# Weights' slots and rows of rounded activations at many places modulo 512 bytes, rows as separate buffers

## What is computed

```python
def swiglu(u, w_gate, w_up, w_down):
    return (jax.nn.silu(u @ w_gate) * (u @ w_up)) @ w_down
for l in range(DEPTH):                      # 2
    x = x + 0.5 * g1 * swiglu(modulate(x, sh1, sc1), ffn1_gate[l], ffn1_up[l], ffn1_down[l])
    x = x + g2 * token_mix(modulate(x, sh2, sc2), cos, sin, w_in[l], ...)
    x = x + 0.5 * g3 * swiglu(modulate(x, sh3, sc3), ffn2_gate[l], ffn2_up[l], ffn2_down[l])
# then hybrid_layer: z = h @ w_in + b_in; four branches; merged @ w_o; relu(h2 @ w_up)**2 @ w_down
```

## Time and profile before

| | |
|---|---|
| median of 3 runs | 3470.61 us (3468.10 to 3471.58) |
| span of the profiled execution, first to last instruction | 3462.0 us |
| median less that span | 8.6 us |
| PE busy, share of the span | 99% |
| DVE, ACT, POOL busy | 51%, 35%, 8% |

### The profile page before, as it was taken

One profiled execution on the slowest core, in us unless ns is written; L12 is line 12 of the kernel. 1 busy time (PEld: TensorE's weight loads), 2 busy tenths in 40 slices (PEclk: granted clock), 3 DMA queues, 4 the chain that ended last, 5 costly groups with the idle time before them and its releaser, 6 DMA issues.

```text
span 3462.0 us, 40836 instructions
## 1 busy us (share of the span) xinstructions
PE 3417.4 (99%) x16686; PEld 2737.1 (79%) x16686; DVE 1754.0 (51%) x3014; ACT 1197.3 (35%) x2021; POOL 263.1 (8%) x219
## 2 busy tenths in 40 slices
PE   8999999999999999999999999999999999999999
PEld 7888786778888788887767888888778777878887
DVE  7666446555565733334655643334453555364433
ACT  3222336543222332223555332224322444233322
POOL 0000210002000200011100100003011000120000
PEclk9999999999999999999999999999999999999999
DMA  7555322123565532323211322322222223122332
GB/s 253 203 208 192 108 84 69 41 71 112 190 228 194 183 100 95 104 86 117 74 44 31 105 90 83 106 87 96 77 79 68 76 67 122 39 96 90 98 103 79
DMA packets 120361, 376.36 MB, mean 109 GB/s; under 512 B 13296, under 2 KB 28272, under 8 KB 120176
## 3 DMA queue, kind: packets, MB, share of 16 engines
q1 hardware_dynamic: 120176, 373.76, 32.8%
HBM read 371.61 MB, written 2.10 MB: 108 GB/s over the span
## 4 chain that ended last, share of the span: by engine, by line
PE 93%; DVE 4%; ACT 2%; issue 0%; DMA 0%; POOL 0%; SPq 0%; DVEq 0%; ACTq 0%; POOLq 0%
PE ps L449 27%; PE ps L451 26%; PE ps L450 26%; PE ps L671 2%; PE ps L694 2%; PE ps L566 2%; PE ps L483 1%; PE ps L485 1%; PE ps L484 1%; PE ps L499 1%; DVE s_wl L1490 1%; PE ps L492 1%; ACT s_wh L969 0%; PE ps L536 0%; PE ps L537 0%
## 5 line engine op out<-in xcount | busy, mean ns | idle before, releaser
L1490 DVE TENSOR_TENSOR s_wl<-s_raw,s_wh 128x1024 fp32r<-128x1024 f32 (+3 forms) x645 | 705.7, 1095 | 885.2 <-ACT s_wh L969 878.7
L449 PE MATMUL ps<-s_uh,s_wh 128*128 128x512 f32 x2824 | 1128.5, 400 | 9.7 <-DVE s_ul L1551 3.8
L451 PE MATMUL ps<-s_ul,s_wh 128*128 128x512 f32 x2824 | 1104.2, 391 | 0.8 <-issue 0.8
L450 PE MATMUL ps<-s_uh,s_wl 128*128 128x512 f32 x2824 | 1103.4, 391 | 0.0
L969 ACT ACTIVATE s_wh<-s_raw 128x1024 fp32r<-128x1024 f32 (+3 forms) x645 | 588.1, 913 | 723.0 <-PE ps L451 535.4
L449 PEld LDWEIGHTS ps<-s_uh,s_wh 128*128 128x128 f32 x2824 | 532.2, 188 | 152.8 <-issue 40.2
L451 PEld LDWEIGHTS ps<-s_ul,s_wh 128*128 128x128 f32 x2824 | 531.7, 188 | 113.6 <-issue 1.2
L450 PEld LDWEIGHTS ps<-s_uh,s_wl 128*128 128x128 f32 x2824 | 532.5, 189 | 107.3 <-issue 2.7
L449 PE MATMUL ps<-s_fh,s_wh 128*128 128x512 f32 x960 | 378.6, 394 | 0.0
L451 PE MATMUL ps<-s_fl,s_wh 128*128 128x512 f32 x960 | 378.6, 394 | 0.0
L450 PE MATMUL ps<-s_fh,s_wl 128*128 128x512 f32 x960 | 378.6, 394 | 0.0
(11 more groups left out here) (419 smaller groups left out, 3337.9 us busy)
## 6 DMA issues: line engine op xcount, KB each, us to landing
s_raw<-w SPq DMA_DIRECT2D x616, 512.0 KB, 3.6
s_raw<-w SPq DMA_DIRECT2D x96, 192.0 KB, 2.4
s_raw<-w SPq DMA_DIRECT2D x64, 256.0 KB, 2.6
s_raw<-w SPq DMA_DIRECT2D x19, 128.0 KB, 2.0
s_x<-x SPq DMA_DIRECT2D x4, 512.0 KB, 6.7
out<-s_x SPq DMA_DIRECT2D x8, 256.0 KB, 2.2
s_raw<-w SPq DMA_DIRECT2D x4, 420.0 KB, 4.2
s_crow<-crow SPq DMA_DIRECT2D x2, 512.0 KB, 6.0
```

The source lines that it names most:

```text
L449: TE.matmul(o, w_hi(i, k), h, start=first, stop=False)
L450: TE.matmul(o, w_lo(i, k), h, start=False, stop=False)
L451: return TE.matmul(o, w_hi(i, k), l, start=False, stop=last)
L1490: V.tensor_tensor(wl[w][:, 0:n], raw[t % NRAW][:, 0:n], wh[w][:, 0:n].bitcast(F32), SUB).then_inc(*s_lo.up(("lo", t)))
```

## The change

The three slots of `wh`, the three of `wl`, and each of the eight rows of `uh` and `ul` become buffers of their own, with small unused buffers (`gap`) between them, so that their places are the numbers in the lists: `wh` 0, 16, 64; `wl` 96, 160, 288; `uh` 288 to 0; `ul` 0 to 320. `Rows` lets the code go on writing `uh[:, k, :]`. `skip(224)` brings the first slot from place 288 to 0. Behind `ul` 7 at 320 the same 960 bytes follow, so `fh`, `fl`, `oAh`, `oBh`, `bh` and their low parts come to 256, and `qh` and `ch` to 384. `lai` and `lfm`, two small buffers of the hybrid layer, share one. Every engine has the same instructions with the same operands, waits and order as before; addresses alone differ.

```diff
--- before.py
+++ after.py
@@ -193,6 +193,17 @@
     memset = affine_select = dma_start = then_inc = op
 
 
+class Rows:
+
+
+    def __init__(self, rows):
+        self.rows = rows
+
+    def __getitem__(self, at):
+        p, k, w = at
+        return self.rows[k][p, w]
+
+
 class Tiles:
 
 
@@ -269,10 +280,29 @@
     cst = sb(top, "cst", [128, ncol])
     x = sb(top, "x", [128, 8, 512])
     raw = [sb(top, f"raw{i}", [128, 1024]) for i in range(NRAW)]
-    wh = [sb(top, f"wh{i}", [128, 1024], F32R) for i in range(NW)]
-    wl = [sb(top, f"wl{i}", [128, 1024], F32R) for i in range(NW)]
-    uh = sb(top, "uh", [128, 8, 512], F32R)
-    ul = sb(top, "ul", [128, 8, 512], F32R)
+    gap = [0]
+
+    def skip(n):
+        if n:
+            gap[0] += 1
+            sb(top, f"gap{gap[0]}", [128, n // 4])
+
+    def spaced(names, width, phases, at):
+        out = []
+        for name, phase in zip(names, phases):
+            skip((phase - at) % 512 // 32 * 32)
+            fine = phase % 32
+            t = sb(top, name, [128, width + fine // 4], F32R)
+            out.append(t[:, fine // 4:fine // 4 + width])
+            at = (phase + 4 * width + 31) // 32 * 32 % 512
+        return out, at
+
+    skip(224)
+    wh, at = spaced([f"wh{i}" for i in range(NW)], 1024, (0, 16, 64), 0)
+    wl, at = spaced([f"wl{i}" for i in range(NW)], 1024, (96, 160, 288), at)
+    uh, at = spaced([f"uh{k}" for k in range(8)], 512, (288, 304, 320, 336, 352, 384, 448, 0), at)
+    ul, at = spaced([f"ul{k}" for k in range(8)], 512, (0, 16, 32, 64, 96, 128, 192, 320), at)
+    uh, ul = Rows(uh), Rows(ul)
     acc = sb(top, "acc", [128, 512])
     tmp = [sb(top, f"tmp{i}", [128, 512]) for i in range(4)]
     mod = sb(top, "mod", [128, 144])
@@ -319,8 +349,9 @@
         with ExitStack() as d:
             lqk = sb(d, "lqk", [128, 8, 512])
             lmo = sb(d, "lmo", [128, 4, 512])
-            lai, lmx = (sb(d, n, [4, 512]) for n in ("lai", "lmx"))
-            lfm = sb(d, "lfm", [36, 512])[32:36, :]
+            lmx = sb(d, "lmx", [4, 512])
+            laf = sb(d, "laf", [36, 512])
+            lai, lfm = laf[0:4, :], laf[32:36, :]
             lsum = sb(d, "lsum", [128, 384])
             lcol = sb(d, "lcol", [128, 4, 4])
             lv = sb(d, "lv", [128, 4, 512])
```

## The result

| | before | after |
|---|---|---|
| median | 3471.10 us (3468.10 to 3481.73, 4 runs) | 3509.64 us (3501.04 to 3512.57, 4 runs) |
| ratio after / before | | 1.009, 95% interval 1.0066 to 1.0115 |
| span of the profiled execution | 3462.0 us | 3508.7 us |

The change made the kernel 0.9% slower, 38.5 us by the medians. The forecast was 3450 us with a range of 3425 to 3495 us: the sign is wrong, and the time is outside the range.

A forecast was written before the change was run, and what follows sets the result against it. The prediction took PE to bound the kernel, matmul count times start-to-start distance. Down and branch products at -27.0 us and all others at +6.6 gave -20.4 us, from 3470.6 to 3450 us, range 3425 to 3495 us.

The forecast's parts named there:

- 213.3 + 13.9: Matmuls other than down and branch products, before: 213.3 ns for 512 columns plus a mean loss of 13.9 ns.
- at 192, 10.0: Loss of 10.0 ns a matmul at gap 192 (moving row's place less loaded weights' place), read from 280-column triples.
- the straight lines: Losses at unmeasured gaps joined linearly: 10.0 to 20.0 ns from 192 to 448, 20.0 to 15.5 from 448 to 0.
- bounds: Other loss curves between gaps 192 and 448: -41 to +11 us; all matmuls at lowest or highest loss: -72 or +56.
- a high far side: Rival, slower: loss reaches 20.0 ns soon behind gap 192, giving +11 us, 3482 us; chance 0.15.
- -27.0: 3,647 down and branch matmuls, moved from gap 448: loss falls from 20.0 to 12.6 ns, saving 27.0 us.
- +6.6: 9,192 other matmuls, mostly `uh` and `ul`: mean loss rises from 13.9 to 14.6 ns, losing 6.6 us.
- no settling: Rival, slower: PE's low distance needs an unchanging gap, which the change prevents; +24 us at 17.5, +42 at 18.9; chance 0.20.
- `s_uh` near 231 ns and `s_fh` near 231 too: Profile sign that the forecast is wrong because distances no longer settle: both matmul groups start about 231 ns apart.
- 8.6 us between span and median: Difference between profiled span and median before, assumed to stay when turning the 3441.6 us span into 3450 us.

The follow-up runs named there:

- the table: 512-column distances in kernels with constant gaps modulo 256: 226.7 ns at 0, 231.7 at 16, 233.3 at 32, 228.9 at 64, 233.4 at 96, 234.2 at 160, 233.3 at 192 and 224.

## Why the prediction was wrong

**What held.** PE bounds the kernel before and after, and the time is matmuls times distance; DVE, ACT and the waits did not move. Places matter, as `fh` against `uh` had shown. The Trainium skill's rules in "TensorE: Matmul & The Clock Gate", part 2, and "SBUF — State Buffer", "Who interferes with whom", by which they couldn't, do not hold here: 226.7 against 233.3 ns for the same down products in windows of clock 1.00, with only the rows' place changed. Which of the two reads gives way, no run shows. The mean before was put at 213.3 + 13.9 = 227.2 ns for the others, and single starts give 227.3.

**The step that failed first** is "at 192, 10.0". A loss read from two triples of 280-column matmuls was taken as the price of a gap at 512 columns. The constant gap 192 costs 20.0 at 512 columns. Nor is the low value at 280 columns shown to belong to gap 192. Over all such starts of the kernel before the means are 130.2 ns at gap 0, 130.8 at 96 and 127.3 at 192, less far apart than in the earlier trace rows; and in the kernel with `uh` and `ul` at 480, where the slots' row `j` = 2 is at gap 0 and no longer at 192, that row still has the lowest mean, 126.8 ns. The kernel with `wl` at 96 shows one way in which such a reading goes astray: a start-to-start time isn't the price of that matmul's own gap. Whether that is all of it is open, since in the earlier trace rows two of the three distances follow a matmul of the same gap.

**The second** is the straight lines, "192 to 448: 10.0 to 20.0; 448 back to 0". 256 was put at 12.5 and is 13.4; 192 and 160 were put at 10.0 and 11.7 and are 20.0 and 20.9; 32, put at 15.5 with its whole range, is 20.0. No smooth line through few points could have found a map with a period of 256 bytes and one deep hole. The "bounds" didn't protect either: "a high far side" let only the gaps behind 192 rise and kept 10.0 at 192.

**The two terms.** "-27.0" for the down and branch products measured -3. By the table five of their six new gaps cost 231 to 234 ns, where the old one cost 233.3, and the sixth didn't keep its low price either: at gap 256 the starts are 233.3 ns apart in the changed kernel (824 starts). "+6.6" for the others measured +43, because nearly all of them left the one cheap gap. With the prices of the table (231.5 for places off 32, 232.4 for gap 128, guessed from its neighbours and the few matmuls there) the change's gaps sum to a mean of 231.6 ns, against 232.1 measured: the map gives nine tenths of the loss without any history. That agreement of the means is no proof of single prices. Grouped by their own gap, the down and branch matmuls of the changed kernel show 233.3 ns at 256, which the table has as cheap, and 231.2 at 192, which it has as dear. And the table misses the `wl` kernel by 2.2 ns. How much of the loss each gap makes by itself and how much its neighbours make stays open; shown is that both count, and that there is no loss where every gap is 0 or 256.

**The rival "no settling"** came nearest in numbers: +24 to +42 us, and its sign in the profile, "`s_uh` near 231 ns and `s_fh` near 231 too" (232 and 232.5). Its mechanism is right only in part. Gaps that change by 256 do settle at 226.7, and the constant gaps 32, 96, 160, 192 and 224 do not settle low at all; true is that a matmul at gap 0 among others is dearer than in a run of its own (234.5 against 226.6 ns). Its chance was too low, because the earlier trace rows was held against it.

**One slip without effect**: the "8.6 us between span and median". Around the profiled execution's span lie 1.7 us (3510.43 less 3508.7 after, the same in the experiments). That profiled execution of before simply ran some 7 us below the median, which is why the spans differ by 46.7 us and the medians by 38.5.

## What to carry to other kernels

In a stream of fp32r matmuls that each load new weights, put the moving rows and the weight tiles at the same address modulo 256 bytes, on multiples of 32: 64 pad bytes were worth 24 us here, 0.7%, by the distances. Before a price is interpolated between operand places, run each place constant over a long stretch; and in a pipelined stream don't charge the distance behind an instruction to that instruction's operands alone. Where most of the work already sits at the best known setting, variety can only take it away, and the few cases at a bad setting are better moved alone.

## What the runs showed of the hardware

- The distance of 512-column fp32r matmuls with a 128 x 128 weight load each depends on the difference of the two operands' addresses: 226.7 ns at 0 and 256, 228.9 at 64, 233.3 to 234.2 at 32, 96, 160, 192, 448 and 480 (all with the weights at 288; gap 0 also with everything at 0 or 320).
- Both operands 16 bytes off a multiple of 32 cost 231.1 ns at gap 0; in other stretches of that kernel it settled at 230.0 or 233.3.
- The distance depends on the neighbours' gaps too: at gap 0, 226.6 ns behind a matmul of gap 0 and 234.5 behind one of gap 32. With gaps 192, 0 and 0 in turn it is 229.2, 235.4 to 235.8 and 228.5 ns.
- Open: what in the memory has steps of 32 and a period of 256 bytes; what the 280-column matmuls, whose moving operand is the weights, go by (126.7 ns at gap 192 and 132.2 at gap 0 in the earlier trace rows, but 126.8 at gap 0 in the kernel with `uh` at 480); whether the gap that counts is the one to the weights loaded beside a matmul or to its own; and the price of a gap in a mixed sequence.
